# Two recurrent and attention mixers on one core: six conditioning items of the first, four of the second, and the first mixer's last steps, in another order

## The reference

```python
cond = jax.nn.silu(c)
mod = cond @ ada_w[i] + ada_b[i]
sh1, sc1, gt1, sh2, sc2, gt2 = jnp.split(mod[:, None, :], 6, axis=-1)
hin = x * (1 + sc1) + sh1
y = mixer(hin)
x = _layernorm(ALPHA * x + (1 + gt1) * y, ln_g[i, 0], ln_b[i, 0])
```

```python
ym = y.mean(-1, keepdims=True)
yv = jnp.square(y - ym).mean(-1, keepdims=True)
yn = ((y - ym) * lax.rsqrt(yv + GN_EPS)) * lnx_g + lnx_b
out = (yn + bonus) * g
return out @ w_out
```

## Time and profile before

| | us |
|---|---|
| median of 3 runs | 1440.94 (1437.32 to 1440.96) |
| the profiled execution, its time | 1444.98 |
| the span of its instructions | 1443.3 |
| PE busy in it | 1356.7 (94%) |
| DVE busy | 910.0 (63%) |
| ACT busy | 672.6 (47%) |
| POOL busy | 216.9 (15%) |

### The profile page before, as it was taken

One profiled execution on the slowest core, in us unless ns is written; L12 is line 12 of the kernel. 1 busy time (PEld: TensorE's weight loads), 2 busy tenths in 40 slices (PEclk: granted clock), 3 DMA queues, 4 the chain that ended last, 5 costly groups with the idle time before them and its releaser, 6 DMA issues. The chain is left out here.

```text
span 1443.3 us, 18455 instructions
## 1 busy us (share of the span) xinstructions
PE 1356.7 (94%) x7264; PEld 1118.1 (77%) x7264; DVE 910.0 (63%) x1255; ACT 672.6 (47%) x964; POOL 216.9 (15%) x123
## 2 busy tenths in 40 slices
PE   6999899699999989999999989989999989989998
PEld 2774579677888877687888868978887878978987
DVE  1686882769778767557765464765554677545564
ACT  2534332255444354536444336564472667326561
POOL 0001541104000041304000000300001342500200
PEclk8999999899999989989999999999999999999999
DMA  9851580067898774544876547834533541018940
GB/s 350 281 174 48 176 292 1 1 202 258 286 308 293 241 208 155 176 146 154 262 226 211 168 127 169 205 114 132 187 134 125 163 146 59 31 48 200 224 143 30
DMA packets 160630, 247.16 MB, mean 171 GB/s; under 512 B 15064, under 2 KB 100028, under 8 KB 160032
## 3 DMA queue, kind: packets, MB, share of 16 engines
q1 hardware_dynamic: 159216, 239.61, 52.9%
q0 software_dynamic: 1328, 6.38, 1.2%
HBM read 244.86 MB, written 4.24 MB: 173 GB/s over the span
## 5 line engine op out<-in xcount | busy, mean ns | idle before, releaser
L199 DVE TENSOR_TENSOR w_lo<-w_raw,w_hi 128x2048 fp32r<-128x2048 f32 (+3 forms) x176 | 403.3, 2298 | 245.3 <-ACT w_hi L190 245.1
L211 PE MATMUL ps<-w_hi,act_hi 128*128 128x512 f32 (+4 forms) x1216 | 471.4, 388 | 15.7 <-DVE act_lo L871 6.2
L213 PE MATMUL ps<-w_hi,act_lo 128*128 128x512 f32 (+4 forms) x1216 | 463.2, 381 | 0.0
L212 PE MATMUL ps<-w_lo,act_hi 128*128 128x512 f32 (+4 forms) x1216 | 462.5, 380 | 0.0
L190 ACT CAST w_hi<-w_raw 128x2048 fp32r<-128x2048 f32 (+3 forms) x176 | 316.9, 1806 | 264.1 <-PE ps L213 213.0
L211 PEld LDWEIGHTS ps<-w_hi,act_hi 128*128 128x128 f32 x1216 | 230.6, 190 | 61.5 <-issue 14.3
L213 PEld LDWEIGHTS ps<-w_hi,act_lo 128*128 128x128 f32 x1216 | 230.1, 189 | 36.2
L212 PEld LDWEIGHTS ps<-w_lo,act_hi 128*128 128x128 f32 x1216 | 230.7, 190 | 35.1 <-issue 1.0
L678 POOL TENSOR_TENSOR nstat<-nstat,con 128x1 f32<-128x1 f32 x8 | 5.4, 680 | 430.4 <-DVE nstat L673 430.4
L211 PE MATMUL ps<-w_hi,ffn_gh 128*128 128x512 f32 x176 | 69.7, 396 | 0.0
L213 PE MATMUL ps<-w_hi,ffn_gl 128*128 128x512 f32 x176 | 68.6, 390 | 0.0
(11 more groups left out here) (508 smaller groups left out, 1829.1 us busy)
## 6 DMA issues: line engine op xcount, KB each, us to landing
w_raw<-in_ffn_w_in SPq DMA_DIRECT2D x88, 512.0 KB, 5.0
w_raw<-in_fox_w_in SPq DMA_DIRECT2D x32, 912.0 KB, 8.9
w_raw<-in_ada_w SPq DMA_DIRECT2D x28, 1024.0 KB, 5.7
w_raw<-in_ffn_w_out SPq DMA_DIRECT2D x20, 1024.0 KB, 5.6
w_raw<-in_rwkv_w_rkv SPq DMA_DIRECT2D x12, 1024.0 KB, 7.0
con<-in_ada_w SPq DMA_DIRECT2D x48, 256.0 KB, 5.4
w_raw<-in_gla_w_in SPq DMA_DIRECT2D x10, 896.0 KB, 4.8
w_raw<-in_gdn_w_in SPq DMA_DIRECT2D x10, 896.0 KB, 4.8
```

The lines of the kernel that those rows point to most:

```text
L199: self.nc.vector.tensor_tensor(lo[:, s, 0:c["nk"], 0:c["width"]], self.raw[:, c["slot"], 0:c["nk"], 0:c["width"]], hi[:, s, 0:c["nk"], 0:c ...
L211: nc.tensor.matmul(out(t)[:, 0:w], xh[:, k, tok], hi[:, s, j, 0:w], start=start, stop=False)
L212: nc.tensor.matmul(out(t)[:, 0:w], xh[:, k, tok], lo[:, s, j, 0:w], start=False, stop=False)
L213: return nc.tensor.matmul(out(t)[:, 0:w], xl[:, k, tok], hi[:, s, j, 0:w], start=False, stop=stop)
```

## The change

In the first mixer: the sixth item is no longer summed in the loop of units but behind the last `y`, and the turns of the fifth and the sixth stand there too. `ada_part` moves to where `m.lw` lay, so ACT waits for `across` (the last matmul that reads it) ahead of the first part. `inv_x` and `sa` move out of slot 0 of the split rings, and the first chunk of `rwkv_out` is split inside the stage: the high half on ACT ahead of `sa(2)`, the low half on DVE behind `variance(1)`. The product with the gate is taken out of `gated` and put ahead of it (`gate`), `gated(1)` goes ahead of `y(2)`, and `dve_cols` goes ahead of the last two `gated`. Four `keep_warm` matmuls stand at PE's end. In the second mixer the four turns are at n = 2, 4, 4 and 6, and `dve_cols` at n = 6.

```diff
-        self.x = [core.place("inv_x", [P, 8, 64], top + 2048 * g) for g in range(2)]
-        self.sa = [core.place("sa", [P, COLS], top + 4096 + 2048 * g) for g in range(2)]
+        lw = core.s0 + 3 * 8192
+        self.ada_at = lw
+        self.x = [core.place("inv_x", [P, 8, 64], lw + 4096 + 2048 * g) for g in range(2)]
+        slot = KG * COLS * 4
+        self.sa = [core.place("sa", [P, COLS], spot) for spot in (core.hi_at + slot, core.lo_at + slot)]
...
+    held = len(items) - 1
...
+    hi, lo = core.rings = core.split_rings()
+    core.ahead["rwkv_out"] = 1
+    ahead = core.jobs["rwkv_out"][0][0]
...
-                    if done < len(items):
+                    if done < held:
                         ada.pe_sums(pe, sem, done)
                     if done == 1:
                         pe.wait_ge(sem("across_e"), 1)
-                    if 1 <= done <= len(items):
+                    if 1 <= done < held:
                         ada.pe_turn(pe, sem, done - 1)
...
             y(2)
             y(3)
-            more(len(items) + 1 - done)
+            ada.pe_sums(pe, sem, held)
+            ada.pe_turn(pe, sem, held - 1)
+            ada.pe_turn(pe, sem, held)
+            core.keep_warm(1, 4)
+            pe.wait_ge(sem("var"), 3)
+            core.keep_warm(3, 4)
...
+            act.wait_ge(sem("across"), 1)
             more(1)
...
             square(1)
+            act.wait_ge(sem("up6_mm"), 4)
+            core.split_hi(act, hi, ahead)
             sa(2)
...
-            more(len(items) - done)
+            ada.act_part(act, sem, held)
...
             variance(1)
+            core.split_lo(dve, hi, lo, ahead)
+            gate(0)
+            gate(1)
             gated(0)
+            gated(1)
             y(2)
             centre(2)
             y(3)
             centre(3)
-            gated(1)
             variance(2)
             variance(3)
+            gate(2)
+            gate(3)
+            ada.dve_cols(dve, sem)
             gated(2)
             gated(3)
-            ada.dve_cols(dve, sem)
...
+    turns = {2: (0,), 4: (1, 2), 6: (3,)}
...
-            if n == 4:
+            if n == 6:
                 pe.wait_ge(sem("ada_cols"), 2)
...
-                if n == 4:
-                    pe.wait_ge(sem("o"), 3)
-                    for i in range(len(items)):
+                if n in turns:
+                    pe.wait_ge(sem("o"), n - 1)
+                    for i in turns[n]:
                         ada.pe_turn(pe, sem, i)
...
-                if n == 4:
+                if n == 6:
                     ada.dve_cols(dve, sem)
```

More of the change, by code:

```diff
@@ L1709, in __init__ @@
         self.lt = core.place("lt", [P, 32, 32], top)
-        self.x = [core.place("inv_x", [P, 8, 64], top + 2048 * g) for g in range(2)]
-        self.sa = [core.place("sa", [P, COLS], top + 4096 + 2048 * g) for g in range(2)]
+        lw = core.s0 + 3 * 8192
[3 more added lines that the diff above has]
+        self.sa = [core.place("sa", [P, COLS], spot) for spot in (core.hi_at + slot, core.lo_at + slot)]
+        assert core.hi_at + slot + 2048 <= m.free + 32768 + 40960 and core.lo_at + slot + 2048 <= top + 8192
         self.inv = core.place("inv", [P, 32, 32], w["rows_at"] + 8192)
@@ L1725, in stage_rwkv_mid @@
     rhs = (m.a[:, 1, :], m.k[:, 1, :])
-    ada = Ada(core, w["ada_at"], items, 6, 7)
+    ada = Ada(core, mm.ada_at, items, 6, 7)
+    held = len(items) - 1
     table = BiasTable(core)
@@ L2154, in variance, with gate @@
                 v.tensor_scalar(var(q), var(q), 1.0 / 64, GN_EPS, ALU.mult, ALU.add).then_inc(sem("var"), 1)
+            def gate(q):
+                t, r_ = rounds[q]
+                out = Y[:, t, half(r_)]
+                if q == 0:
+                    dve.wait_ge(sem("gl"), 1)
+                dve.wait_ge(sem("square"), q + 1)
+                v.tensor_tensor(out, out, gl[:, t, half(r_)], ALU.mult).then_inc(sem("gated"), 1)
             def gated(q):
@@ L2159, in gated @@
                 dve.wait_ge(sem("rstd"), q + 1)
-                dve.wait_ge(sem("square"), q + 1)
+                dve.wait_ge(sem("gated"), q + 1)
                 v.tensor_tensor(by_head(out), by_head(out), bc_in(var(q), 64), ALU.mult).then_inc(sem("out"), 1)
[L2162 to L2166, removed]
+                dve.wait_ge(sem("out"), 2 * q + 1)
                 v.tensor_tensor(out, out, bvg[:, t, half(r_)], ALU.add).then_inc(sem("out"), 1)
```

## The result

| | us |
|---|---|
| before, median of 9 runs | 1442.65 (1437.32 to 1448.06) |
| changed, median of 9 runs | 1432.26 (1430.04 to 1437.05) |
| ratio | 0.9934, interval 0.9917 to 0.9951 |
| span of the profiled execution | 1434.4, before 1443.3 |
| PE busy in it | 1355.4, before 1356.7 |

By the ratio the change brings 9.5 us (7.1 to 12.0). A second measurement of the two kernels gave 0.9902 (0.9877 to 0.9926). A ratio uses the runs of a kernel that lie within 1.5% of its fastest; of all the kernels here only three_turns has others, two of its six.

The account below looks back on a forecast made before the run. PE, its waits and its half-clock spells were taken as the bound, with DVE bounding the first mixer's tail. Gains 3.4 + 1.6 + 6.5 = 11.5 us gave a 1429.4 median; predicted 1429.5, range 1425.5 to 1436.5.

Parts of the forecast that it names:

- The loop of units: First mixer: one sum and two turns leave the loop, gain 3.4 us, bounds 2.5 and 3.8.
- the 0.3: Loop of units: 0.3 us estimated for ACT's copies of kv, which must be out before the next kv.
- DVE would not end last: Before `turn_up`: DVE's last step for the inverses is 4.9 us ahead, more than the 3.8 taken out.
- ACT's cast: First mixer: the first chunk's high half, 1.90 us, goes where ACT had waited 7.71 us and costs nothing.
- DVE's tail: End of first mixer: DVE's steps after variance(1) make 16.5 us without a wait, ending at 281.6, not 283.1.
- PE's tail: End of first mixer: moved sum, turns and four `keep_warm`, partly at low clock, end at 283.3; PE is last.
- The seam: After the first mixer's barrier: 6.37 us to the first `w_out` product becomes 4.6; gain 1.6, bounds 0.5 and 3.7.
- The late chunks: Second and third chunk of `rwkv_out`, asked for at about 273 instead of 207, are covered by some 4 us.
- The attention: Second mixer with its seam: spreading the four turns gains 6.5 us, bounds 0 and 8.3.
- I expect the clock to fall there once more: Attention, at two turns together behind a 1.4 us wait: about 3.5 us at half clock, 1.8 us lost.
- The 8.3 at full clock everywhere: Attention and its seam: terms for turns, logits, transposes, wait, last values and seam total 8.3 us if the clock stays full.
- The rival of the clock that never falls: First mixer's tail and attention: clock stays full in both, gains 3.4 + 3.7 + 8.3 = 15.4, time 1425.5; chance 0.10.

Follow-up runs that it names:

- three_turns: Changed kernel without tail and seam `keep_warm`, ACT's sixth part ahead of `square(3)`, and second-mixer turns at n = 4, 4, 4, 6: 0.9881 of before.
- attend_only: Kernel before with only the second mixer's part: turns at n = 2, 4, 4, 6 and `dve_cols` at n = 6; 0.9964 of before, 5.2 us faster.
- warm_turns: Kernel before, with two unused matmuls of 192 columns ahead of each of the attention's four turns at n = 4: 0.9993 of before.
- mixer_only: Changed kernel with the attention's edits undone, its four turns together at n = 4: 0.9955 of before, 6.5 us faster.
- across_spread: Changed kernel without the tail's `keep_warm`, the 32 `across` records done in pieces of 8 in the loop of turns and b Grams: 0.9924 of before.

## Why the prediction was right, and where not

The forecast was 11.5 us in a median; the ratio gives 9.5 (7.1 to 12.0) the first time and 14.2 (10.7 to 17.8) the second. Part of the agreement is luck: the terms measured in this pair of profiles add up to 15.1, not 11.5, and 6.1 us were lost elsewhere. By its steps:

**The loop of units**, 3.4: measured 3.7, with the wait of 0.19 for ACT's copies that the 0.3 stood for. From PE's first matmul of the stage to the first `turn_up` the three profiles with the long loop take 69.7 to 72.9 us (median 71.1), the ten with the short loop and `across` in one piece 65.9 to 70.6 (67.5). But the first `turn_up` was forecast at 214.2 and stood at 218.50. The step that failed is the tacit one that what lies ahead of an edit stays as it was. Over all profiles the first `turn_up` is at 215.9 to 217.7 in the three with the long loop, and at 208.9 to 214.5 in the ones with the short loop besides the changed kernel's first. That DVE would not end last was right, but the cover is used up: its last step ends 1.35 us ahead of the `turn_up` at 218.50, where it was 4.9.

**ACT's cast** ahead of `sa(2)` cost nothing:

```profile
261.70 1.90 ACT L190 CAST w_hi<-w_raw 128x2048 fp32r<-128x2048 f32 x1 [3.78 <-PE ps L1817]
265.63 0.58 ACT L1987 COPY sa<-ps 128x512 f32<-128x512 f32 x1 [2.03 <-PE ps L1817]
```

ACT still waited 2.03 us behind it. **DVE's tail**, 16.5: from 265.96 to 281.85 it is 15.9, without a wait. **PE's tail**: the sixth turn was forecast 5.0 us behind the last `y` and came 4.6 behind; PE holds the barrier, as forecast, and its `keep_warm` took 5.38 us, the 5.4 of the forecast (277.9 to 283.3). The clock was low for about 3.4 of them, by its mean of 0.57 over 4 us (forecast 3.5). It was still at 1.00 in the wait and the turns ahead, where the forecast had it fall:

```profile
279.00:281.00 2.00, 2.00 (x4) 0.80 (x3) 1.97 (x5) 0.00 (x0) 1.40 (x1) 0.57 1.01 373
281.00:283.00 2.00, 2.00 (x3) 0.72 (x3) 0.82 (x2) 0.00 (x0) 0.00 (x0) 0.57 0.00 0
```

From the end of the last `y` to the seam it is 11.15 us, where the forecast had 11.7 (271.9 to 283.6). The seam took 3.95, not 4.6: 1.78 for the transposes from start to start instead of 2.0, 2.18 for its `keep_warm` instead of 2.6. These two, 0.5 and 0.65, are the terms that were sized wrong, so tail and seam gave 2.8, not 1.6. The late chunks never made ACT wait.

**The attention**, 6.5 with its seam, bounds 0 and 8.3: measured 8.6. The failed step is "I expect the clock to fall there once more". Two turns in a row, behind a wait of 1.42 us, did not bring it down in any of the nine profiles that have the turns of the change; the attention took 34.40 or 34.41 us each time. The 8.3 at full clock everywhere were near the measured 8.6: 1.14 for the logits, 3.68 for the last values, 5.61 for the seam. Only the turns were priced too high, 4.2 for four, where two in a row take 1.83 from start to start. But the size of what is removed isn't one number: with four turns together the attention took 38.5, 42.4 and 45.9 us in three profiles, so the gain is 4.1 to 11.5 by the execution, and in the median of the times 5.2 (attend_only).

**The rival of the clock that never falls** (1425.5) was right for the attention and wrong for the tail. If only waits cost the clock, turns in pieces would bring no more than the wait of 1.15 us; attend_only brought 5.2 (3.2 to 7.2), and warm_turns held the clock with more columns, and with that wait nearly as before (0.99). The Trainium skill (TensorE: Matmul & The Clock Gate, "Why this matters for your kernels") names the gaps between bursts as what costs the clock. Two falls here agree, those of mixer_only behind a wait of 1.42 us and of across_spread in one of 5.29; but a wait of 1.41 or 1.42 us stands at this place in all 14 profiles, and in the 13 others the clock held behind it up to the first turn. The fall of before in `across`, with PE busy for 7.00 of 7.00 us, is not covered by it.

## What to carry to other kernels

Look at the granted clock in the windows, not only at who is busy. Where 32 records with one moving column stood together, the clock fell in all 13 profiles with `across` in one piece and in all three with four bare turns in a row (in one of these already ahead of them). In the one profile with `across` in pieces it did not fall there, nor in any of the 11 in which the turns stood in pieces of up to three or had columns between them. Put such matmuls in pieces between others that stream columns, one where PE would wait. But look first at who ends last in that stretch: where it is another engine, as DVE in across_spread, what PE saves becomes a wait. Where the clock falls in some executions only, divide the profiles at the same instructions and compare those stretches, over several kernels that share the code; one profile against another mixes the edit's gain with differences elsewhere (here 6.1 us against 15.1 of gain).

## What the runs showed that I had not expected

The stretches at the lower clock begin at other points in each execution of the same code: the attention of before took 38.5 to 45.9 us, and the stretch from `turn_up` to the seam 65.7 to 67.2. The times of one kernel go with it: the changed kernel ran 1430.04 us at a mean clock of 0.984 and 1437.05 at 0.976. Where the clock did not fall, a stretch took the same time in each execution: 34.40 or 34.41 us in nine profiles of six kernels.
